# Moving the three slots of the split weights by 0, 64 and 256 bytes within the partition

## The reference, cut to what matters

```
def reference(x, c, ...):
    for l in range(2):
        mod = silu(c) @ ada_w[l] + ada_b[l]
        h = rms_norm(x) * (1 + sc_m) + sh_m
        y = hybrid_mixer(h, ...)     # one input projection, gated gMLP and latent attention, output projection
        x = x + g_m * rms_norm(y)
        h = rms_norm(x) * (1 + sc_f) + sh_f
        y = swiglu(h, ...) if l == 0 else moe_swiglu(h, ...)   # (silu(h @ w1) * (h @ w3)) @ w2
        x = x + g_f * rms_norm(y)
```

## Time and profile before

| What | Value |
|---|---|
| median of 3 runs | 1611.07 us |
| the profiled execution, its time | 1613.58 us |
| its span, first to last instruction | 1611.8 us |
| TensorE matmuls busy | 1537.8 us, 95% |
| TensorE weight loads busy | 1328.5 us, 82% |
| VectorE busy | 1352.7 us, 84% |
| ScalarE busy | 1007.1 us, 62% |
| GpSimd busy | 70.7 us, 4% |
| mean granted TensorE clock | 0.983 |
| moved by the transfers | 507.48 MB, 315 GB/s over the span |

### The profile page before, as it was taken

One profiled execution on the slowest core, in us unless ns is written; L12 is line 12 of the kernel. 1 busy time (PEld: TensorE's weight loads), 2 busy tenths in 40 slices (PEclk: granted clock), 3 DMA queues, 4 the chain that ended last, 5 costly groups with the idle time before them and its releaser, 6 DMA issues.

```text
span 1611.8 us, 21543 instructions
## 1 busy us (share of the span) xinstructions
PE 1537.8 (95%) x8256; PEld 1328.5 (82%) x8256; DVE 1352.7 (84%) x1245; ACT 1007.1 (62%) x861; POOL 70.7 (4%) x99
## 2 busy tenths in 40 slices
PE   3999989999899998999999999999999999999995
PEld 3899979999789977888888887888887888888884
DVE  6987787775778867899899898899898899998885
ACT  3573443433456344777777777777777777777773
POOL 6000000000000000000000000000000000000000
PEclk9999999999999998999999999999999999999998
DMA  9957657775574862999999999999999999999990
GB/s 375 365 182 259 244 229 288 287 254 191 180 251 173 303 221 105 360 384 358 404 374 358 395 381 361 375 380 366 395 375 352 384 376 368 392 376 365 410 368 28
DMA packets 72705, 507.48 MB, mean 315 GB/s; under 512 B 8096, under 2 KB 8224, under 8 KB 13856
## 3 DMA queue, kind: packets, MB, share of 16 engines
q1 hardware_dynamic: 68528, 491.40, 79.8%
q0 software_dynamic: 4080, 14.69, 3.1%
HBM read 499.24 MB, written 6.82 MB: 314 GB/s over the span
## 4 chain that ended last, share of the span: by engine, by line
PE 89%; DVE 6%; ACT 2%; issue 1%; POOL 1%; DMA 0%; DVEq 0%; ACTq 0%; POOLq 0%
PE ps L1348 28%; PE ps L1350 27%; PE ps L1349 27%; PE ps L1744 1%; DVE lo L849 1%; DVE r L901 1%; PE ps L1387 1%; DVE lo L880 1%; DVE ada_acc L813 1%; PE ps L1511 1%; PE ps L1494 1%; PE ps L1367 1%; DVE x_tok L936 1%; DMA router_bias<-in_router_bias_dram 0%; ACT hi L515 0%
## 5 line engine op out<-in xcount | busy, mean ns | idle before, releaser
L880 DVE TENSOR_TENSOR lo<-raw,hi 128x2048 fp32r<-128x2048 f32 x336 | 764.8, 2290 | 96.9 <-ACT hi L515 96.4
L515 ACT ACTIVATE hi<-raw 128x2048 fp32r<-128x2048 f32 x336 | 644.8, 1919 | 200.4 <-PE ps L1350 200.4
L1348 PE MATMUL ps<-hi,hT_hi 128*128 128x512 f32 (+2 forms) x1088 | 428.9, 394 | 11.8 <-DVE hT_lo L907 4.8
L1350 PE MATMUL ps<-hi,hT_lo 128*128 128x512 f32 (+2 forms) x1088 | 420.8, 387 | 0.0
L1349 PE MATMUL ps<-lo,hT_hi 128*128 128x512 f32 (+2 forms) x1088 | 420.2, 386 | 0.0
L1348 PEld LDWEIGHTS ps<-hi,hT_hi 128*128 128x128 f32 x1088 | 205.2, 189 | 56.5 <-issue 8.4
L849 DVE TENSOR_TENSOR lo<-raw,hi 128x2048 fp32r<-128x2048 f32 (+2 forms) x87 | 190.1, 2190 | 62.0 <-ACT hi L499 60.6
L1350 PEld LDWEIGHTS ps<-hi,hT_lo 128*128 128x128 f32 x1088 | 205.1, 188 | 41.1
L1349 PEld LDWEIGHTS ps<-lo,hT_hi 128*128 128x128 f32 x1088 | 205.5, 189 | 38.2 <-issue 0.5
L1348 PE MATMUL ps<-hi,bT_hi 128*128 128x512 f32 (+1 forms) x576 | 226.7, 394 | 1.8 <-DVE bT_lo L1259 1.8
L499 ACT ACTIVATE hi<-raw 128x2048 fp32r<-128x2048 f32 (+2 forms) x87 | 158.3, 1824 | 108.5 <-PE ps L1350 105.4
(11 more groups left out here) (259 smaller groups left out, 1227.5 us busy)
## 6 DMA issues: line engine op xcount, KB each, us to landing
raw<-in_moe_w_dram SPq DMA_DIRECT2D x336, 1024.0 KB, 7.1
raw<-in_w_ada_dram SPq DMA_DIRECT2D x48, 1024.0 KB, 5.2
raw<-in_w_fg_dram SPq DMA_DIRECT2D x11, 1024.0 KB, 5.3
raw<-in_w_fu_dram SPq DMA_DIRECT2D x11, 1024.0 KB, 5.1
raw<-in_w_fd_dram SPq DMA_DIRECT2D x11, 1024.0 KB, 5.7
raw<-in_w_ga_dram SPq DMA_DIRECT2D x8, 1024.0 KB, 6.8
raw<-in_w_gb_dram SPq DMA_DIRECT2D x8, 1024.0 KB, 5.5
raw<-in_w_ab_dram SPq DMA_DIRECT2D x8, 1024.0 KB, 4.9
```

What stands on the lines that cost most here:

```text
L515: act.activation(hi[:, s, :], raw[:, slot, :], ACT.Copy).then_inc(hi_done, 1)
L880: dve.tensor_tensor(lo[:, s, :], raw[:, slot, :], hi[:, s, :].bitcast(f32), ALU.subtract).then_inc(raw_done, 1)
L1348: pe.matmul(o, wh, mh, start=first, stop=False)
L1350: return pe.matmul(o, wl, mh, start=False, stop=last)
```

## The change

The tiles `hi` and `lo` lose their slot dimension and get 128 elements (512 bytes) more. A slot's place within them is now its old place plus `SHIFT`, which is 0, 16 or 64 elements, that is 0, 64 or 256 bytes, for slots 0, 1 and 2. Every instruction that wrote or read `hi[:, slot, ...]` or `lo[:, slot, ...]` takes it through the helper `split`. The number of slots, the sizes, the semaphores and the order of all instructions stay as they are. `raw` stays in its place, `lo` begins 512 bytes later than before, and all tiles behind it begin 1024 bytes later.

```diff
 NRAW, NSPLIT = 7, 3
+SHIFT = (0, 16, 64)
...
-        hi = sb("hi", [P, NSPLIT, CH], f32r)
-        lo = sb("lo", [P, NSPLIT, CH], f32r)
+        hi = sb("hi", [P, NSPLIT * CH + P], f32r)
+        lo = sb("lo", [P, NSPLIT * CH + P], f32r)
...
+        def split(tile, s, e=CH):
+            at = (s % NSPLIT) * CH + SHIFT[s % NSPLIT]
+            return tile[:, at:at + e]
...
-                act.activation(hi[:, s % NSPLIT, 0:e], raw[:, r % NRAW, 0:e], ACT.Copy).then_inc(hi_done, 1)
+                act.activation(split(hi, s, e), raw[:, r % NRAW, 0:e], ACT.Copy).then_inc(hi_done, 1)
...
-                    act.activation(hi[:, s, :], raw[:, slot, :], ACT.Copy).then_inc(hi_done, 1)
+                    act.activation(split(hi, s), raw[:, slot, :], ACT.Copy).then_inc(hi_done, 1)
...
-                dve.tensor_tensor(lo[:, s % NSPLIT, 0:e], raw[:, r % NRAW, 0:e], hi[:, s % NSPLIT, 0:e].bitcast(f32),
+                dve.tensor_tensor(split(lo, s, e), raw[:, r % NRAW, 0:e], split(hi, s, e).bitcast(f32),
                                   ALU.subtract).then_inc(raw_done, 1)
...
-                    dve.tensor_tensor(lo[:, s, :], raw[:, slot, :], hi[:, s, :].bitcast(f32), ALU.subtract).then_inc(raw_done, 1)
+                    dve.tensor_tensor(split(lo, s), raw[:, slot, :], split(hi, s).bitcast(f32), ALU.subtract).then_inc(raw_done, 1)
...
-                return hi[:, s % NSPLIT, :], lo[:, s % NSPLIT, :]
+                return split(hi, s), split(lo, s)
...
-                    return hi[:, (NW + c) % NSPLIT, :], lo[:, (NW + c) % NSPLIT, :]
+                    return split(hi, NW + c), split(lo, NW + c)
...
-                    wh, wl = hi[:, (NW + n) % NSPLIT, :], lo[:, (NW + n) % NSPLIT, :]
+                    wh, wl = split(hi, NW + n), split(lo, NW + n)
```

More of the change, by code:

```diff
@@ L511, in item_hi @@
                 for c in range(lo_c, hi_c):
-                    slot, s = (NR + c) % NRAW, (NW + c) % NSPLIT
+                    slot, s = (NR + c) % NRAW, NW + c
                     act.wait_ge(raw_full[slot], i * (16 * PER_ITEM // NRAW) + 16 * ((NR + c) // NRAW + 1))
                     act.wait_ge(used, i * PER_ITEM + (NW + c - NSPLIT + 1))
-                    act.activation(hi[:, s, :], raw[:, slot, :], ACT.Copy).then_inc(hi_done, 1)
+                    act.activation(split(hi, s), raw[:, slot, :], ACT.Copy).then_inc(hi_done, 1)
             roots, xs = [0], [0]
```

## The result

| | kernel before | changed kernel |
|---|---|---|
| median of 5 runs | 1611.07 us (1609.09 to 1613.02) | 1622.86 us (1620.82 to 1626.32) |
| ratio | 1 | 1.0077, 95% interval 1.0059 to 1.0095 |
| span of the profiled execution | 1611.8 us | 1619.1 us |

The account below looks back on a forecast made before the run. The prediction took TensorE to bound the kernel, with 89% of the chain, then slots. All its terms were 0, so the sum was 0 and the forecast the median of the runs, 1611 us, range 1606 to 1617.

Parts of the forecast that it names:

- The count of the experts' 100 us: TensorE from 1000 to 1100 us: 423 long and 36 short matmuls plus group delays explain 99.9 us of 100.
- TensorE's reads: 0, from the count above: TensorE's operand reads from the shifted slots: the change was to cost 0 us.
- rival B: 512-column products: shifted slots meet other engines' accesses at worse places, 7.3 ns a product, 23 us, 1634 us; chance 0.04.
- its neighbours passed at all distances: Argument against rival B: slow loads are rare, the counted 100 us leaving 0.1 for all, though accesses met at every distance.
- the slow load of rows 10: Load from 720.96 to 723.30 us: 10 steps of 0.234 us, 7 ns over the usual, taken as evidence for rival B.
- Rival A: TensorE's 13.3 ns gap per step belongs to equal places and goes in two of three slots: 32 us faster, 1579; chance 0.03.
- The zeros for the subtraction, the copy, the waits and the tiles behind: VectorE's subtraction, ScalarE's copy, instructions and waits, and the tiles moved by 1024 bytes: each forecast at 0 us.
- What would show it wrong: Signs against the forecast, among them fewer than 455 matmuls in 100 us of the experts at clock 1.00 for rival B.

Follow-up runs that it names:

- the sweep: TensorE alone without the computation, others silent, operand starts shifted in 16-byte steps: 226.6 ns a 512-column step at 0, 256 and 512 bytes, 228.9 to 236.8 elsewhere.
- the versions with 192 and 64 bytes: Against the kernel before: slots 8448 bytes apart, loads used as stationary operand 192 or 64 bytes further; 1607.03 us (ratio 0.9968) and 1606.89 us (0.9955).

## Why the prediction was wrong

**The count of the experts' 100 us** was right, and so was the step of 226.7 ns. What I drew from it was not. "Nothing is left over that could be called a conflict of addresses" holds for the layout that was there. Counted from `raw`, slots, `hT_hi`, `hT_lo`, `bT_hi` and `bT_lo` all started at multiples of 8192 or 1024 bytes, so every product of 512 or 256 columns on a slot stood at one and the same difference, 0 modulo 256 bytes. The rows could not show what another difference costs. A quantity that never varies in the rows that are read is not shown to be harmless by them. (In 48 of the 96 products of 288 columns, whose blocks lie 1152 bytes apart, the difference was 128 bytes. They took 133.3 ns a step like their neighbours, 13.3 over their columns, so they would have given no warning.)

**The step that failed** is the term "TensorE's reads: 0, from the count above". It measured 43 to 50 ns a load in two slots of three, 10.4 us in the experts and 11.0 in all. Behind it stands the argument against rival B, that "its neighbours passed at all distances". That is so for ScalarE, VectorE and the transfers, which start at any time, and they indeed cost nothing (5.51 us with all of them and without). It is not so for the neighbour I left out, TensorE's own load of the next stationary operand, whose record starts together with that of a stream (both at 1000.44 us above). B had the right place (the 512-column products, the chain, no cover, felt from 1 ns) and the wrong partner. Its price of 7.3 ns in two of three slots, 23 us, was too high: the mean is 43 to 50 ns per 12 products, 3.6 to 4.2 ns a step. I gave it 0.04. Its one piece of evidence, the slow load of rows 10, was no conflict with other engines at all. Its steps are 260, 235, 233, 236, 224, 231, 236, 228, 232, 231, 227 and 227 ns, and a silent group at difference 0 in the sweep (705.72 us), behind its first step of 314, has 235, 233, 236, 224, 231, 236, 228, 233, 231, 226 and 227: it is TensorE settling after a short stop (the load for its first product starts at 720.88 us, 0.15 us behind the stream that it otherwise starts with).

**The rule of the Trainium skill** ("SBUF — State Buffer", section "Who interferes with whom") that TensorE never waits for another engine agrees with the runs: 5.44 us at shift 0 in silence and with all at work. But the table of the same section calls TensorE's two read ports, moving operand and weight load, independent. If that is to mean that the place of one operand can't slow the other, the measurement decides against it: moving the stationary operand by 64 bytes alone brings a group from 5.44 to 5.60 us. I read the rule as covering the whole question, when it speaks only of other engines.

**Rival A** took the 13.3 ns over the columns for something that places could change, and that has a grain of truth where I gave none: with 256 columns the gap is 6.7 ns at the good places (113.4 - 106.7). With 512 columns no place was better than the old one. Its count of 1824 products of 256 columns left out those with `bT_hi` and `bT_lo`, 2208 in all; with them its gain outside the experts would have been 26 us instead of 22.

**The zeros for the subtraction, the copy, the waits and the tiles behind** were right: 2292 and 1920 ns, ScalarE's wait 206.4 us for 200.4, and 0.9992 for the tiles alone. **What would show it wrong** was set too wide: "fewer than 455 matmuls in 100 us" missed a loss of 0.7%, as 456 were counted. The length of a single load of 12 products, 2.76 or 2.77 us for 2.72, tells it at once.

## What to carry to other kernels

Where TensorE is the bound and 512 columns stream, keep the starts of its moving and stationary float32r operands (the rounded type) at the same place modulo 256 bytes, and beware of padding that breaks it. With 256 columns another place can be better, as the versions with 192 and 64 bytes show. Then measure the step from start to start, since neither a busy share nor the engine's durations show it. An argument from a trace that nothing is lost needs a look at whether the cause varied. And a disturbance can be paid by the work that follows it: slot 2 was slow for what stood in slot 1.

## What the runs showed of the hardware that was not expected

TensorE's step with float32r operands depends on the difference of its two operands' starts with a period of 256 bytes: 226.6 ns at 0 and 228.9 to 236.8 elsewhere for 512 columns; 120.0 at 0, down to 113.4 at 192 bytes and up to 120.3 elsewhere for 256 columns. That holds where all parts of an operand are moved alike; with single parts moved, the difference to the next stationary operand alone doesn't give the step (231 to 233 ns where it is 0). After a disturbance at a good difference the steps take six to ten products to settle (318, 231, 236, 228, 233, 231, then 226.7), and 64 bytes with 256 columns settled at 117.8 ns in one group and at 113.4 in another. That the two reads meet in the memory is a reading that fits in the main; what happens inside was not measured.
